# Twelve weight products moved from a hosting stage into the row stage before it

## The reference

```python
# second block: the modulation rows of a layer; w is [1024, 6144]
def ada_mod(cvec, w, b):
    return jnp.split(jax.nn.silu(cvec) @ w + b, 6, axis=-1)
...
# first block, layer 0's expert layer, then layer 1's attention (mixer_c)
        y = hier_moe(tok, moe_w_grp[l], ...)
        x = layer_norm(DEEPNORM_ALPHA * x + g2x[:, None, :] * y[:bn * t].reshape(bn, t, d), ln2_g[l], ln2_b[l])
...
        ux = x * (1.0 + s1x[:, None, :]) + sh1x[:, None, :]
...
    q, k, v = split_sizes(z @ w_qkv, C_SPLITS)
```

## Time and profile before

| what | value |
|---|---|
| median of the three runs | 2934.74 us (2934.29 to 2938.98) |
| the profiled execution, its own time | 2944.24 us |
| its span | 2942.4 us |
| TensorE busy | 2419.4 us (82%) |
| VectorE busy | 650.6 us (22%) |
| ScalarE busy | 368.3 us (13%) |
| DMA | 724.53 MB, mean 246 GB/s |
| DMA share of the 16 engines, main queue | 59.0% |

### The profile page before, as it was taken

One profiled execution on the slowest core, in us unless ns is written; L12 is line 12 of the kernel. 1 busy time (PEld: TensorE's weight loads), 2 busy tenths in 40 slices (PEclk: granted clock), 3 DMA queues, 4 the chain that ended last, 5 costly groups with the idle time before them and its releaser, 6 DMA issues. The chain is left out here.

```text
span 2942.4 us, 35137 instructions
## 1 busy us (share of the span) xinstructions
PE 2419.4 (82%) x14539; PEld 1311.1 (45%) x14539; DVE 650.6 (22%) x1420; ACT 368.3 (13%) x648; POOL 122.6 (4%) x170
## 2 busy tenths in 40 slices
PE   7999888998888866984688788885566999767998
PEld 3333564444344333333343233333244776654775
DVE  2000467310000014006532100003342000262000
ACT  0000312111111111003221011010031000200000
POOL 0000010000000011000100000001000000000000
PEclk9999978999999987997889999997788999887999
DMA  8888512899999966770189999993402444412442
GB/s 294 322 296 304 190 47 78 348 423 423 423 423 423 422 255 245 278 271 36 53 339 421 423 422 423 423 387 132 135 10 69 153 157 149 145 43 84 153 157 72
DMA packets 180210, 724.53 MB, mean 246 GB/s; under 512 B 14453, under 2 KB 72693, under 8 KB 114464
## 3 DMA queue, kind: packets, MB, share of 16 engines
q1 hardware_dynamic: 165664, 674.14, 59.0%
q0 software_dynamic: 8512, 25.83, 2.7%
q10 hardware_dynamic: 5952, 23.42, 2.2%
HBM read 699.04 MB, written 23.25 MB: 245 GB/s over the span
## 5 line engine op out<-in xcount | busy, mean ns | idle before, releaser
L1871 PE MATMUL bank<-ring,arena 128*64 128x512 f32 x1632 | 378.5, 613 | 72.6 <-DMA ring<-moe_w_up 46.5
L438 PE MATMUL bank<-ring,actT 128*128 128x512 f32 x768 | 346.9, 605 | 5.4 <-DMA ring<-c_w_qkv 3.0
L2246 PE MATMUL bank<-actT,ring 128*128 128x256 f32 x1408 | 308.8, 380 | 2.2 <-PEq L524 2.2
L2246 PEld LDWEIGHTS bank<-actT,ring 128*128 128x128 f32 x1408 | 268.4, 191 | 47.3 <-issue 11.6
L1500 PE MATMUL bank<-arena 128*64 128x512 f32 x1088 | 242.8, 599 | 25.3 <-ACT arena L1568 23.3
L1871 PEld LDWEIGHTS bank<-ring,arena 128*64 128x64 f32 x1632 | 115.8, 140 | 329.9 <-issue 216.6
L438 PEld LDWEIGHTS bank<-ring,actT 128*128 128x128 f32 x768 | 143.6, 192 | 208.4 <-issue 208.4
L1860 PEld LDWEIGHTS bank<-arena 128*128 128x128 bf16 x5280 | 160.5, 99 | 33.9 <-issue 29.0
L1608 DVE TENSOR_TENSOR arena<-arena,bank 128x512 f32<-128x512 f32 x34 | 23.4, 688 | 662.5 <-ACT arena L1566 662.5
L1860 PE MATMUL bank<-arena 128*128 128x64 bf16 x5280 | 164.9, 195 | 5.6 <-DVE arena L1600 4.3
L2260 PE MATMUL bank<-ring,arena 128*128 128x512 f32 x352 | 154.3, 592 | 0.0
(11 more groups left out here) (358 smaller groups left out, 1949.7 us busy)
## 6 DMA issues: line engine op xcount, KB each, us to landing
ring<-moe_w_gate SPq DMA_DIRECT2D x136, 1024.0 KB, 24.1
arena<-moe_w_down SPq DMA_DIRECT2D x136, 1024.0 KB, 21.4
ring<-ada_w SPq DMA_DIRECT2D x96, 1024.0 KB, 7.3
ring<-moe_w_up SPq DMA_DIRECT2D x68, 1024.0 KB, 24.3
actT<-moe_w_up SPq DMA_DIRECT2D x68, 1024.0 KB, 24.7
ring<-ffn_w SPq DMA_DIRECT2D x66, 1024.0 KB, 5.3
made_scratch<-arena ACTq DMA_DIRECT2D x34, 512.0 KB, 7.8
ring<-ab_w_in SPq DMA_DIRECT2D x14, 1024.0 KB, 8.1
```

The lines of the kernel that those rows point to most:

```text
L438: mm = nc.tensor.matmul(self.bank[g % 6][:, :], lhsT(m, k), halves[k // 4][:, k % 4, :], start=(k == 0), stop=(k == KT - 1))
L1871: return self.nc.tensor.matmul(self.bank[j // 2][64 * i:64 * i + 64, :], xs[:, S * kt:S * kt + S], piece[:, k * DE:(k + 1) * DE], start=(k ...
L2246: mm = nc.tensor.matmul(bank[2 * (j % 2) + which][:, f * SEQ:(f + 1) * SEQ], w[:, k, f * P:(f + 1) * P], self.actT[:, k * T:k * T + SEQ], ...
```

## The change

The first twelve of the 32 units (round 0 whole, and four units of round 1) are done by TensorE in the row stage of the first expert layer, three ahead of each tile's transposes. They are also the first twelve loads of the plan, ahead of the first c_w_qkv chunk. The remaining twenty are spread over the 20 groups of the hosting stage, one each. Banks 6 and 7 belong to the rounds from the row stage on, so the row stage's transposes use three pairs of banks in turn, and the fourth tile's wait until ScalarE has emptied the first pair (`zT_ready`). Round 0's bias is added by VectorE behind group 0 of the hosting stage (`over`). The product itself, `ada_product`, is the old code under a name of its own.

```diff
--- before.py
+++ after.py
@@ -39,6 +39,7 @@
 AB_ROUNDS = [(0, 1), (0, 2), (1, 0), (1, 1), (1, 2), (2, 0), (2, 1)]
 C_CHUNKS = [[0, 1]] * 2 + [[0, 1, 2, 3]] * 4
 C_ROUNDS = [(2, 2), (3, 0), (3, 1), (3, 2)]
+C_LEAD = 12
 KT = D // P
 SEQ = 256
 T = 2 * SEQ
@@ -370,10 +371,12 @@
 
         return [(g + 1) * n // groups - g * n // groups for g in range(groups)]
 
-    def plan_hosting(self, w, chunks, rounds):
-
-        share = self.spread(8 * len(rounds), sum(len(tiles) for _, tiles in chunks))
+    def plan_hosting(self, w, chunks, rounds, lead=0):
+
+        share = self.spread(8 * len(rounds) - lead, sum(len(tiles) for _, tiles in chunks))
         units = [(l, r, k) for l, r in rounds for k in range(KT)]
+        for _ in range(lead):
+            self.plan_ada(*units.pop(0))
         g = 0
         for c, tiles in chunks:
             self.plan_linear(w, c, c + 512)
@@ -387,14 +390,28 @@
         w = (self.I["ada_w"], self.I["ada_w_2"])[l // 2][l % 2]
         self.plan(w[k * P:(k + 1) * P, 2048 * r:2048 * (r + 1)].rearrange("(k p) n -> p k n", p=P), 1, 2048)
 
-    def st_linear_hosting(self, lhsT, chunks, dest, rounds, unmix=None, tables=None):
+    def ada_product(self, pe, n, l, r, k):
+
+        self.arrived(pe, self.used)
+        sl = self.slot(self.used)
+        for j in range(4):
+            mm = self.nc.tensor.matmul(self.bank[6 + n % 2][32 * j:32 * j + 32, :],
+                                       self.scx[:, 256 * (l // 2) + 32 * k:256 * (l // 2) + 32 * k + 32],
+                                       sl[:, 0, 512 * j:512 * j + 512], start=(k == 0), stop=(k == KT - 1))
+        c = self.sem["ada_done"] if k == KT - 1 else self.weights_used
+        mm.then_inc(c.up(), 1)
+        self.frees(self.used, c)
+        self.used += 1
+
+    def st_linear_hosting(self, lhsT, chunks, dest, rounds, lead=0, unmix=None, tables=None):
 
 
 
         nc, sm = self.nc, self.sem
         groups = [(ci, m) for ci, tiles in enumerate(chunks) for m in tiles]
-        share = self.spread(8 * len(rounds), len(groups))
-        units = [(n, l, r, k) for n, (l, r) in enumerate(rounds) for k in range(KT)]
+        share = self.spread(8 * len(rounds) - lead, len(groups))
+        units = [(n, l, r, k) for n, (l, r) in enumerate(rounds) for k in range(KT)][lead:]
+        over = lead // KT
         after, at = [], 0
         for n in share:
             after.append(units[at:at + n])
@@ -413,16 +430,7 @@
                 def ada(n, l, r, k):
                     if k == 0 and n >= 2:
                         pe.wait_ge(ada_added.sem, ada_added.at(n - 1))
-                    self.arrived(pe, self.used)
-                    sl = self.slot(self.used)
-                    for j in range(4):
-                        mm = nc.tensor.matmul(self.bank[6 + n % 2][32 * j:32 * j + 32, :],
-                                              self.scx[:, 256 * (l // 2) + 32 * k:256 * (l // 2) + 32 * k + 32],
-                                              sl[:, 0, 512 * j:512 * j + 512], start=(k == 0), stop=(k == KT - 1))
-                    c = ada_done if k == KT - 1 else self.weights_used
-                    mm.then_inc(c.up(), 1)
-                    self.frees(self.used, c)
-                    self.used += 1
+                    self.ada_product(pe, n, l, r, k)
 
                 g = 0
                 for tiles in chunks:
@@ -495,11 +503,11 @@
                     if g % 2:
                         dve.wait_ge(self.pe_done.sem, self.pe_done.at(g + 1))
                         nc.vector.tensor_copy(dest(*groups[g]), self.bank[g % 6][:, :]).then_inc(self.dve_done.up(), 1)
-                    for n, l, r, k in after[g]:
-                        if k == KT - 1:
-                            dve.wait_ge(ada_bias.sem, ada_bias.at(64 * (n + 1)))
-                            dve.wait_ge(ada_done.sem, ada_done.at(n + 1))
-                            nc.vector.tensor_tensor(kept, self.bank[6 + n % 2][:, :], kept, ALU.add).then_inc(ada_added.up(), 1)
+                    for n in [n for n in range(over) if g == n] + [n for n, l, r, k in after[g] if k == KT - 1]:
+                        dve.wait_ge(ada_bias.sem, ada_bias.at(64 * (n + 1)))
+                        if n >= over:
+                            dve.wait_ge(ada_done.sem, ada_done.at(n + 1 - over))
+                        nc.vector.tensor_tensor(kept, self.bank[6 + n % 2][:, :], kept, ALU.add).then_inc(ada_added.up(), 1)
 
     def load_mod(self, sp, l, lo, hi, vecs):
 
@@ -1723,6 +1731,8 @@
         nc, A, bank, stat, sm = self.nc, self.A, self.bank, self.stat, self.sem
         row = lambda r, t: A(t * D if r == 0 else ZP + t * 2048 if nt == 2 else ZP + t * D, D)
         stat_ready, z_ready, z_turned, x_normed, row_scaled = (sm[n] for n in ("stat_ready", "z_ready", "z_turned", "x_normed", "row_scaled"))
+        zT_ready = sm["zT_ready"]
+        to_bank = lambda n, g: bank[2 * (n % 3 if layer == 0 else n) + g]
         turns = list(range(4)) if layer == 0 else [2, 3, 0, 1]
         put = self.put_mixed if layer == 0 else self.put_pure
         source = lambda t: A(CTX[t - 2], D) if layer and t >= 2 else row(0, t)
@@ -1747,13 +1757,19 @@
 
             @block.tensor
             def _(pe):
+                ahead = [(n, l, r, k) for n, (l, r) in enumerate(C_ROUNDS) for k in range(KT)][:C_LEAD]
                 for n, t in enumerate(turns):
+                    if layer == 0:
+                        for _ in range(C_LEAD // 4):
+                            self.ada_product(pe, *ahead.pop(0))
+                        if n >= 3:
+                            pe.wait_ge(zT_ready.sem, zT_ready.at(2 * (n - 3) + 2))
                     if t < nt:
                         pe.wait_ge(z_ready.sem, z_ready.at(t + 1))
                     for g in range(2):
                         for q in range(4):
                             k = 4 * g + q
-                            mm = nc.tensor.transpose(bank[2 * n + g][:, q * P:(q + 1) * P], source(t)[:, k * P:(k + 1) * P], self.ident)
+                            mm = nc.tensor.transpose(to_bank(n, g)[:, q * P:(q + 1) * P], source(t)[:, k * P:(k + 1) * P], self.ident)
                         mm.then_inc(z_turned.up(), 1)
 
             @block.scalar
@@ -1765,7 +1781,7 @@
                 for n, t in enumerate(turns):
                     for g in range(2):
                         act.wait_ge(z_turned.sem, z_turned.at(2 * n + g + 1))
-                        nc.scalar.activation(put(t, g), dims(bank[2 * n + g][:, :], [P, 4], [1, P]), ACT.Copy)
+                        nc.scalar.activation(put(t, g), dims(to_bank(n, g)[:, :], [P, 4], [1, P]), ACT.Copy).then_inc(zT_ready.up(), 1)
 
             @block.sync
             def _(sp):
@@ -2003,7 +2019,7 @@
         def dest(c, t):
             base = (QR, K, V)[c // 2]
             return A(base + t * D + 512 * (c % 2), 512)
-        self.st_linear_hosting(lambda m, k: self.actT[:, k * T + m * P:k * T + m * P + P], C_CHUNKS, dest, C_ROUNDS, unmix=A(XX, 2048))
+        self.st_linear_hosting(lambda m, k: self.actT[:, k * T + m * P:k * T + m * P + P], C_CHUNKS, dest, C_ROUNDS, lead=C_LEAD, unmix=A(XX, 2048))
         LQ = XX + 2048 + 256
         LAM = LQ + 2048
         with self.stage() as block:
@@ -2450,7 +2466,7 @@
         self.plan_linear(I["ab_w_in"][0], 3584, 3616, ks=8)
         self.plan_linear(I["ab_w_out"][0], 0, D)
         self.plan_experts(0)
-        self.plan_hosting(I["c_w_qkv"][0], [(512 * n, tiles) for n, tiles in enumerate(C_CHUNKS)], C_ROUNDS)
+        self.plan_hosting(I["c_w_qkv"][0], [(512 * n, tiles) for n, tiles in enumerate(C_CHUNKS)], C_ROUNDS, C_LEAD)
         self.plan_linear(I["c_w_out"][0], 0, D)
         self.plan_experts(1)
         w = I["a_w_in_2"][0]
```

## The result

The changed kernel takes 2943.25 us (median of 13 executions, 2940.64 to 2950.16) against 2935.73 for the kernel before, timed together with it (13, 2930.86 to 2941.97): a ratio of 1.0029, interval 1.0020 to 1.0037. It is slower, by 7.5 us between the medians (5.9 to 10.9 by the interval); forecast were +4.2 us and no change within 0.2%. In both kernels the executions differ among themselves by some 10 us.

A forecast was written before the change was run, and what follows sets the result against it. DMA was taken to bound the row stage and TensorE the hosting stage. +20.8 - 10.3 - 4.7 - 1.6 = +4.2 us gave 2938.9 us, no change within 0.2%; range 2932.5 to 2943.7.

The forecast's parts named there:

- The later start (+20.8): Hosting stage's first matmuls wait for the fourteenth load, starting at 1151.4 in place of 1130.59: +20.8 us.
- the rival's deciding point of 2.65: Row stage: spacing of load landings, in us, from which a stream below 422 GB/s decides for slower; chance 0.24.
- Twelve units (-10.3): Hosting stage: twelve units fewer, each 0.86 us, leaving one unit per group, 161.2 us for 20 groups: -10.3 us.
- The hole and its cold group (-4.7): Hosting stage: the wait for the second w_qkv chunk and the slow group behind it disappear: -4.7 us.
- The clock of the first group: Hosting stage: first group starts cold as before, 0 us change; warm start, chance 0.26, would give -2.9 us.
- The rope stage (-1.6): After the hosting stage: 1 MB less queued ahead of the rope stage's parameters, so its wait shortens: -1.6 us.
- the bound of 0.2%: Whole kernel: a difference up to 5.9 us counts as no change; chance of the same 0.67.
- slow stream: Row stage: loads land 2.89 us apart at 363 GB/s, +9.0 us in all, 2943.7; chance 0.24.
- The rival from the Trainium skill: Row stage: HBM to SBUF bound near 358 GB/s, 2.93 us a load, fourteenth at 1156.7, total 2944.2; no separate chance.

The follow-up runs named there:

- loads alone: Changed kernel with all twelve early loads, but nine of the twelve products compute only 32 of 512 columns; ratio 1.0036 to the kernel before.
- products alone: Changed kernel without the twelve early loads, the products reading modulation rows already in place; ratio 0.9944 to the kernel before.
- The other order of units: Kernel before, all 32 units in the hosting stage, but one unit each behind groups 0 and 1; ratio 0.9998.
- the earlier feed: Changed kernel, SyncE waiting for the rows of two tiles, not four, in the first expert layer's row stage before feeding the ring; ratio 0.9984.

## Why the prediction was wrong

**The later start (+20.8): right in kind, sized 1.1 low.** Measured are 39.2 - 17.35 = +21.9 (mean of the profiles). SyncE's wait stayed, the products were free and the fourteenth landing set the start, as the runs with loads alone and products alone show. The landings were (1150.08 - 1116.0) / 13 = 2.62 us apart in the mean, and not 2.5. Up to the ninth they were 2.49 apart, as forecast; the tenth came 3.7 us after the ninth (3.7 to 4.0 in the four profiles), and the last four were 2.63 apart. DMA did not rest there: the ring's queue had moved 9.9 MB when the ninth load was in (nine loads are 9.4 MB), 11.4 at the tenth (10.5) and 15.7 at the fourteenth (14.7). So more of the loads behind had gone before the one that was waited for; why from the tenth on, no run shows. The mean spacing is near the rival's deciding point of 2.65, but its mechanism, a stream of 363 GB/s and landings 2.89 apart, was not there.

**Twelve units (-10.3): right.** Groups are 8.06 apart throughout. With four units ahead the hosting stage came out at 168.1, to the tenth what the beat gives (12 x 8.06 + 8 x 8.92).

**The hole and its cold group (-4.7): this step failed.** It was read from one profile and carried into the sum as if each execution had it. Three of five profiles have it and pay 4.7, 6.3 and 4.8 us for it with its cold group, two pay nothing: 3.1 in the mean. Together with the first group's clock the hosting stage ranges from 171.5 to 180.2, mean 176.9. After the change it is 163.2 in the mean, so the stage gave back 13.7 and not 15.0. The other order of units, without a hole in its profile, gained nothing that could be measured: 0.9998 (0.9986 to 1.0010), where a hole in each execution asks for 0.9984. The profile that the sum stood on was itself 9.5 us over the median; the prediction said so and took the step to be the same in both. If a usual execution is shorter than the five profiles, as estimated above, the stage gave back less still.

**The clock of the first group.** Cold was taken, and of four profiles three show 8.8 us and one 9.96 against 7.13 warm: 1.6 to 2.8 of the 2.9. Before was cold in four profiles of five. Right in kind.

**The rope stage (-1.6): right.** 22.3 became 20.4 in the mean, -1.9, with three c_w_out loads out in time. The other kernels bear it out: 20.3 us in the two further ones with one unit behind the last group and twelve loads, 20.3 without the loads, and 22.2 to 22.4 in the six with two units behind the last group.

**The sum.** 21.9 - 13.7 - 1.9 - 0.3 (gather to rows) = +6.0 by the means, against +4.2. Of the gap of 1.8, +1.1 is the spacing of landings, +1.3 the hosting stage and -0.6 the two small stretches. That is little, but the forecast lay 1.7 us below the bound of 0.2%, and so both together turned "no change" into "slower". The timing has +7.5 us, 1.5 more than the sums; where this lies is not shown. The chance of 0.24 for slower hung on a slow stream alone; the chance that before's profile was not typical had no price in it, and it pointed the same way. That 2943.25 us still lies within the range, up to 2943.7, is luck: that end was priced by the slow stream, which did not come.

**The rival from the Trainium skill** (DMA: Bandwidth & Descriptors, Specifications): about 358 GB/s for a core would have put the start, by the prediction's estimate, at 43 us after the rows. The trace has 39.2 us at a mean of 401 GB/s over the row stage, and doesn't agree with it as a bound.

**Two shorter versions.** Four units ahead: the loads end with the rows' chain, the products fill the same holes, and the hosting stage loses the hole. Its two timings are 0.9991 (0.9975 to 1.0008) and 0.9983 (0.9972 to 0.9995); the second is faster than before beyond its interval, the first is not. Twelve units with the earlier feed come to 0.9984 (0.9971 to 0.9997). Both are clearly faster than the changed kernel; against the kernel before the gain is 0.1 to 0.2% and just clear of the scatter in two timings of three.

## What to carry to other kernels

Work that is moved into an idle engine's holes brings its loads along. Count their landings from the first instant at which the loads may be issued; the next stage's own loads land behind them, and the last of these is its start. Of the three numbers tried here the best was the one whose last load landed when the stage's other chain ended: four and not twelve. A wait of a few microseconds that one profile shows beside other traffic may be a matter of chance: before it is booked as a gain, profile several executions, above all when the profiled one is slower than the median.

## What the runs showed of the hardware

A 1 MB weight load that was issued within a microsecond of GpSimd's four residual transfers took 8.5 to 12.3 us to land; with none beside it, it took 5.8. Over the landing of load 7 in the first profile of before (1141.7 to 1153.5) DMA was 98% busy at 266 GB/s, against 422 GB/s with weight loads only the earlier trace rows. A fourth tile's gathered rows came 8.4 us later when SyncE's stream of weight loads ran beside the gathers. And the hosting stage of one and the same kernel took 171.5 to 180.2 us from execution to execution, in steps that its timeline names: a first group of 7.1 or 9.4 to 10.1 us, and a hole of 3.0 to 3.5 us with a third group of 8.8 to 10.0 us behind it, or neither.
